# Retention's gated output: its five turnings placed in the seventh and eighth step and in front of the branch projection

## The chip, the cores and the metric

The kernel runs on one core of a Trainium2 chip. The metric is device time in microseconds (us) of one execution. The core has a matrix engine (TensorE, PE in the profile, its weight loads PEld), a vector engine (VectorE, DVE), an activation engine (ScalarE, ACT), GpSimd (POOL) and a queue that issues transfers (SyncE, SP). They run on their own instruction streams, in order, and wait for each other by semaphores. TensorE writes only to PSUM, which has eight banks of 128 partitions x 512 float32; the other engines read the results there and free the bank.

## The reference

One layer of a hybrid encoder trunk: a combined input projection, retention with four heads, differential attention, a mixture of experts. The change touches retention alone, for 512 prompt rows and 8 x 16 sample rows (640 rows, five tiles of 128):

```python
rq, rk = rope(q), rope(k) * RET_DK ** -0.5           # 4 heads, 256 columns each
ret_o, ret_state_new = retention(rq, rk, rv, state)  # 512 value columns per head
ret_o = rms_norm(ret_o) * silu(rg)                   # per head, gated
merged = sigmoid(gates)[ret] * (ret_o @ w_br_ret) + sigmoid(gates)[diff] * (diff_o @ w_br_diff)
```

`ret_o` of a head is 640 x 512. For the product with `w_br_ret` (the branch projection) it must stand with its 512 columns on the partitions, so it is transposed ("turned"), tile by tile. The norm's factor of each row is applied after the product.

## The kernel before

A float32 product is made of three matmuls (`mm3`, L93 to L95) of high and low parts in a rounded format, so each operand is split: ACT makes the high part, another engine the low part. Weights come by DMA into a ring of four pieces of 256 rows (`load_piece`), ACT makes the high part (L628), GpSimd the low part (L546).

`project` multiplies the 640 rows by one group of 512 weight columns: eight steps (one per 128 rows of the contraction), each of five tiles x three matmuls, into the five banks `pj[0]` to `pj[4]`. In front of step i it calls `between(i)`, which issues other work of PE. The stage runs, for each head h: QKh (columns of q and k), then the branch projection of the head before (`BR{h-1}`), then Vh (values), Gh (gate), the products inside the head (`values`) and `state`. For h = 4, the last round, the columns of the merging gate (GR0) stand in the place of QK. BR has two halves "a" and "b" of four steps, each with its own five banks' worth of results, so bank t must be emptied of QK's tile t before the first step of half a touches it (`pj_free`).

Small results of PE go by turns into two scratch banks (`sm`, named r_sm in the trace). They are numbered jobs: a job may start when the job two before it has been taken (`small`, `sm_free`). The list of jobs is written out in `retention_order`, and PE's program must issue them in that order: around the change it is one unit of the modulation (AD), the state products U8 to U15, the five turnings O0 to O4, and two more units inside BR.

While PE runs QK (or GR0), `in_qk` gives it: at step i = 1 a modulation unit and the rest of the sample rows' product with the state (`cross`); at i = 2 to 5 two state products each (`steps`, L1094); at i = 5 behind them turning 0; at i = 6 turnings 1 and 2; at i = 7 turnings 3 and 4. So "the sixth step" is i = 5, "the eighth" i = 7. `turn_o(h, t)` is four transposes of 128 x 128 (L1111) from `gate[:, t]` into one scratch bank. `in_branch` issues a modulation unit at steps 1 and 5 of BR.

DVE takes the state products U (`update`, L853), gates the sample tile, computes the sums for the norm, then `lo_oT` for t = 0 to 4 (L867: the low part of turned tile t, which frees the scratch bank), five small instructions of a reciprocal root, in rounds 1 to 3 the rotation of three tiles of the new q and k, and then `add_branch` (L886, L888), which empties the banks of half a.

ACT's program in a round is an order written out by hand:

```python
split_hi(b, 0)
take_oT(h - 1, 0)
take_oT(h - 1, 1)
act.wait_ge(var_done, h)
act.activation(st[:, 2, 0:NT], st[:, 1, 0:NT], ACT.Sqrt).then_inc(std_done, 1)
split_hi(b, 1)
take_oT(h - 1, 2)
take_oT(h - 1, 3)
split_hi(b, 2)
take_oT(h - 1, 4)
...
take(first, lambda t: qk[:, t].rearrange("p a c -> p (a c)"), ACT.Copy)   # ACT.Sigmoid in the last round
```

`take_oT(h, t)` (L667) is the high part of turned tile t; `take` (L633) empties the five banks of QK (or GR0), tile by tile. The lines L686 to L711 hold this order. SP loads the branch's piece p when QK's piece p has been used. "Second head" is the round with h = 2, from 290 us on; "last head" is the round with h = 4.

Of the kernel before, what the change touches and what calls it, by code (L numbers as in the profile page):

```python
# [41 lines left out]
NP_T = SEQ // P  # L42
# [48 lines left out]
def mm3(pe, out, s_hi, s_lo, m_hi, m_lo, start, stop):  # L91

    pe.matmul(out, s_hi, m_hi, start=start, stop=False)  # L93
    pe.matmul(out, s_hi, m_lo, start=False, stop=False)  # L94
    return pe.matmul(out, s_lo, m_hi, start=False, stop=stop)  # L95
# [102 lines left out]
def phase_r(nc, io, K):  # L198
# [9 lines left out]
    with ExitStack() as ctx:  # L208
# [23 lines left out]
        oT_hi = sb("r_oT_hi", [P, 4, NT * P], F32R)  # L232
        oT_lo = sb("r_oT_lo", [P, 4, NT * P], F32R)
# [81 lines left out]
        def job_taken(eng, *job):  # L315
            eng.wait_ge(sm_free[o.job[job] % 2], o.job[job] // 2 + 1)
# [10 lines left out]
        def bank_taken(eng, name, t):  # L327
            eng.wait_ge(pj_free[t], o.turn[name, t] + 1)
# [621 lines left out]
        def _(pe):  # L950
# [48 lines left out]
            def small(*job):  # L999
                n = o.job[job]  # L1000
                if n >= 2:
                    pe.wait_ge(sm_free[n % 2], n // 2)
                return sm[n % 2]

            def project(name, stat_hi, stat_lo, between):
                parts = [("", range(KT))] if name[:2] != "BR" else [("a", range(4)), ("b", range(4))]
                for part, ks in parts:
                    for k in ks:
                        i = k + (4 if part == "b" else 0)
                        p, kk = i // 2, i % 2  # L1010
                        between(i)
                        if kk == 0:
                            pe.wait_ge(lo_done, o.piece[name, p] + 1)
                        if name == "QK0":
                            pe.wait_ge(h_lo, k + 1)
                        for t in range(NT):
                            if name == "QK0":
                                in_start(k, t)
                            if k == 0:
                                turn = o.turn[name + part, t]  # L1020
                                if turn:
                                    pe.wait_ge(pj_free[t], turn)
                                if part:
                                    job_taken(pe, "O", int(name[-1]), t)
                            s = slice(t * P, (t + 1) * P)
                            last = mm3(pe, pj[t][:], stat_hi[:, k, s], stat_lo[:, k, s], hi[:, p, kk], lo[:, p, kk],
                                       k == 0, k == ks[-1])
                            if k == ks[-1]:
                                last.then_inc(pj_done, 1)
                        if kk and k != ks[-1]:  # L1030
                            last.then_inc(used, 1)

            def unit(u):
                out = small("AD", u)
                pe.wait_ge(u_in, 16 * (u + 1))
                for k in range(KT):
                    j = k % NH
                    last = pe.matmul(out[32 * j:32 * j + 32, 0:UW], cS[:, k], uraw[:, k], start=(k < NH), stop=(k >= KT - NH))
                last.then_inc(sm_done, 1)
# [19 lines left out]
            def values(h, i):  # L1059
                name = f"AV{h}"  # L1060
                if o.turn[name, i]:
                    pe.wait_ge(pj_free[i], o.turn[name, i])
                pe.wait_ge(sc_low, h + 1)
                for j in range(i + 1):
                    bank_taken(pe, f"V{h}", j)
                    b = scoff[j] // P + i - j
                    high = qk_r[:, b // 2, 0, b % 2 * P:(b % 2 + 1) * P]
                    last = mm3(pe, pj[i][:], high, sc_lo[:, b * P:(b + 1) * P], v_hi[:, j], v_lo[:, j], j == 0, j == i)
                last.then_inc(pj_done, 1)
# [8 lines left out]
            def cross(h, q):  # L1078
                d = q // 2
                pe.wait_ge(z_done, h * 5 + d + 1)  # L1080
                pe.wait_ge(S_in[q % 2], 64 * (h * 2 + d + 1))
                for u in range(4 * q, 4 * q + 4):
                    j = strip(u)
                    last = pe.matmul(X[32 * j:32 * j + 32], qz[:, d, stream(u)[1]], S[:, u % 8], start=False, stop=(q == 3))
                if q == 3:
                    last.then_inc(x_done, 1)

            def steps(h, u0):
                pe.wait_ge(vk_in, 128 * (h + 1))
                for u in (u0, u0 + 1):  # L1090
                    (a, s), d = place_of(u), u // DEC_B
                    out = small("U", h, u)
                    k0 = K_AT[s] + d * P
                    pe.matmul(out[:], vk[:, a, k0:k0 + P], vk[:, a, RDK:RDK + RDV], start=True, stop=True).then_inc(sm_done, 1)  # L1094

            def state(h, d):
                out = small("S", h, d)
                pe.wait_ge(kd_low, h + 1)
                for t in range(NP_T):
                    s = slice(d * P, (d + 1) * P)  # L1100
                    last = mm3(pe, out[:], kd_hi[:, t, s], qk_r[:, t, 1, s], v_hi[:, t], v_lo[:, t], t == 0, t == NP_T - 1)
                last.then_inc(sm_done, 1)

            def turn_o(h, t):
                if t < NP_T:
                    bank_taken(pe, f"AV{h}", t)
                else:
                    pe.wait_ge(x_free, h + 1)
                out = small("O", h, t)
                for a in range(4):  # L1110
                    last = pe.transpose(out[:, a * P:(a + 1) * P], gate[:, t, a * P:(a + 1) * P], K.ident[:])  # L1111
                last.then_inc(sm_done, 1)

            def in_start(k, t):
                if k == 0:
                    turned_x(pe, NT + t)
                if (k, t) in ADA_AT:
                    ada(1 + ADA_AT.index((k, t)))
                elif (k, t) in TURN_AT:
                    turn_mod(1 + TURN_AT.index((k, t)))  # L1120

            def in_qk(h, u, i):
                if i == 1:
                    unit(u)
                    cross(h, 2)
                    cross(h, 3)
                elif 2 <= i <= 5:
                    steps(h, 4 + 2 * i)
                if i == 5:
                    turn_o(h, 0)  # L1130
                elif i == 6:
                    turn_o(h, 1)
                    turn_o(h, 2)
                elif i == 7:
                    turn_o(h, 3)
                    turn_o(h, 4)

            def in_branch(u, i):
                if i % 4 == 1:
                    unit(u + i // 4)  # L1140

            def in_v(h, i):
                if i >= 3:
                    turn_qk(h, ROPE_ORDER[i - 3])

            def in_gate(h, u, i):
                if i == 0:
                    scores(h, 4)
                elif i == 1:
                    scores(h, 0)  # L1150
                elif i == 2:
                    sample_values(h)
                    unit(u)
                    cross(h, 0)
                    cross(h, 1)
                    scores(h, 1)
                elif i == 3:
                    scores(h, 2)
                    scores(h, 3)
                elif i >= 5:  # L1160
                    steps(h, 2 * i - 10)
# [12 lines left out]
            u = 0  # L1174
            for h in range(RH + 1):
                if h == 0:
                    project("QK0", *hT, lambda i: None)
                else:
                    project(f"QK{h}" if h < RH else "GR0", *hT, lambda i: in_qk(h - 1, u, i))
                    project(f"BR{h - 1}", oT_hi, oT_lo, lambda i: in_branch(u + 1, i))  # L1180
                    u += 3
                if h == RH:
                    break
                project(f"V{h}", *hT, lambda i: in_v(h, i))
                project(f"G{h}", *hT, lambda i: in_gate(h, u, i))
                u += 1
                for i in range(NP_T):
                    values(h, i)
                    if i == 0:
                        steps(h, 6)  # L1190
                state(h, 0)
                state(h, 1)
# [1879 lines left out]
```

## Time and profile before

| | |
|---|---|
| median of 3 runs | 1493.19 us (1491.91 to 1493.68) |
| the profiled execution's own time | 1492.03 us |
| its span | 1489.8 us |
| PE busy | 1461.5 us (98%) |
| DVE, ACT, POOL busy | 837.7 (56%), 659.5 (44%), 303.2 us (20%) |
| retention stage | from the start to about 700 us of the span |
| waits of PE from 150 to 640 us | 2.8 + 0.6 us, all at L1111 |

Matmuls overlap: each is recorded with 0.39 us, and the next starts 0.23 us after it. So times on PE are read from start to start, and a step of fifteen matmuls is 3.4 us. "[0.71 <-DVE r_S L853]" behind a row is the idle time of the engine before it, and what ended it. "x4" merges four instructions that follow each other.

### The profile page before, as it was taken

How to read it: one execution, taken by the hardware profiler on the slowest of the kernel's cores; microseconds unless marked ns; L12 is line 12 of the kernel's file. 1: busy time of each engine (PE TensorE's matmuls, PEld its weight loads, DVE VectorE, ACT ScalarE, POOL GpSimd, SP SyncE). 2: the span in 40 equal slices, each digit the busy share in tenths (PEclk: the TensorE clock that was granted, in tenths of full speed). 3: DMA queues.
4: the chain of work that ended last, by engine and by line, in shares of the span. 5: the costliest groups of instructions: out<-in, count | busy, mean ns of one | idle time of the engine just before them, and what ended most of it. 6: DMA issues, size and time to landing. Idle time of an engine off the chain costs nothing.

```text
span 1489.8 us, 21889 instructions
## 1 busy us (share of the span) xinstructions
PE 1461.5 (98%) x8004; PEld 1158.5 (78%) x8004; DVE 837.7 (56%) x1456; ACT 659.5 (44%) x1083; POOL 303.2 (20%) x181
## 2 busy tenths in 40 slices
PE   8999999999999999999999999999999999999998
PEld 6777787778777877787877677777888888887885
DVE  3532532253225222221866778655365899988998
ACT  5323312331233123322446545645233478888883
POOL 1352233224313431233000000000321100001004
PEclk9999999999999999999999999999999999999999
DMA  9646565555556455433441353245831799999996
GB/s 324 216 125 204 170 192 140 187 191 184 158 185 208 144 167 197 161 99 91 159 142 43 111 168 133 71 153 178 276 124 43 267 372 404 403 365 402 399 393 230
DMA packets 156460, 304.61 MB, mean 204 GB/s; under 512 B 16752, under 2 KB 54520, under 8 KB 155972
## 3 DMA queue, kind: packets, MB, share of 16 engines
q1 hardware_dynamic: 152548, 292.72, 58.2%
q0 software_dynamic: 3808, 10.49, 2.0%
q8 instruction: 66, 1.08, 0.3%
q14 instruction: 38, 0.31, 0.1%
HBM read 258.45 MB, written 47.86 MB: 206 GB/s over the span
## 4 chain that ended last, share of the span: by engine, by line
PE 45%; DMA 4%; DVE 2%; issue 1%; ACT 1%; POOL 0%; DVEq 0%; ACTq 0%; SPq 0%; POOLq 0%
PE pj L93 11%; PE pj L95 11%; PE pj L94 11%; DMA m_raw<-w 2%; PE d_B L2731 1%; PE d_B L2758 1%; PE d_B L2750 1%; DMA d_kc<-cache_diff_k 1%; PE d_B L2792 1%; PE d_B L2740 1%; PE d_B L2898 1%; PE d_B L2719 1%; PE d_B L1762 1%; PE d_B L2769 0%; PE pj L1745 0%
## 5 line engine op out<-in xcount | busy, mean ns | idle before, releaser
L93 PE MATMUL pj<-ring_hi,hT_hi 128*128 128x512 f32 x880 | 364.1, 414 | 3.7 <-ACT d_q_rows L2193 2.4
L95 PE MATMUL pj<-ring_hi,hT_lo 128*128 128x512 f32 x880 | 345.2, 392 | 0.0
L94 PE MATMUL pj<-ring_lo,hT_hi 128*128 128x512 f32 x880 | 344.0, 391 | 0.0
L546 POOL TENSOR_TENSOR ring_lo<-ring_raw,ring_hi 128x1024 fp32r<-128x1024 f32 x79 | 190.7, 2414 | 462.6 <-ACT ring_hi L628 462.5
L1622 DVE TENSOR_TENSOR m_lo<-m_raw,m_hi 128x1024 fp32r<-128x1024 f32 x188 | 222.1, 1221 | 18.8 <-ACT m_hi L1528 17.3
L628 ACT ACTIVATE ring_hi<-ring_raw 128x1024 fp32r<-128x1024 f32 x79 | 83.5, 1059 | 313.8 <-DMA ring_raw<-w_in 272.8
L1528 ACT ACTIVATE m_hi<-m_raw 128x1024 fp32r<-128x1024 f32 x188 | 192.0, 1058 | 19.9 <-DMA m_raw<-w 17.8
L93 PEld LDWEIGHTS pj<-ring_hi,hT_hi 128*128 128x128 f32 x880 | 166.2, 189 | 41.8 <-issue 8.9
L95 PEld LDWEIGHTS pj<-ring_hi,hT_lo 128*128 128x128 f32 x880 | 165.4, 188 | 36.1
L94 PEld LDWEIGHTS pj<-ring_lo,hT_hi 128*128 128x128 f32 x880 | 166.4, 189 | 29.3 <-issue 1.0
L853 DVE SCALAR_TENSOR_TENSOR r_S<-r_S,g,r_sm 128x512 f32<-128x512 f32 x64 | 45.0, 745 | 128.4 <-PE r_sm L1094 128.4
L93 PE MATMUL pj<-m_hi,m_xT_hi 128*128 128x512 f32 x248 | 98.4, 397 | 0.8 <-DVE m_lo L1622 0.8
L95 PE MATMUL pj<-m_hi,m_xT_lo 128*128 128x512 f32 x248 | 96.9, 391 | 0.0
L94 PE MATMUL pj<-m_lo,m_xT_hi 128*128 128x512 f32 x248 | 96.6, 390 | 0.0
L2186 ACT ACTIVATE ring_hi<-ring_raw 128x1024 fp32r<-128x1024 f32 x37 | 39.1, 1058 | 66.4 <-DMA ring_raw<-w_in 27.2
L1492 POOL DMA_INDIRECT m_xe<-xg,m_si x16 | 19.8, 1239 | 229.0 <-PE d_B L1754 209.6
L93 PE MATMUL pj<-ring_hi,r_oT_hi 128*128 128x512 f32 x160 | 63.4, 396 | 0.0
L94 PE MATMUL pj<-ring_lo,r_oT_hi 128*128 128x512 f32 x160 | 62.5, 391 | 0.0
L95 PE MATMUL pj<-ring_hi,r_oT_lo 128*128 128x512 f32 x160 | 62.3, 389 | 0.0
L841 DVE COPY r_qkT<-r_sm 128x512 f32<-128x512 f32 x20 | 13.8, 691 | 75.9 <-PE r_sm L1045 75.9
L93 PEld LDWEIGHTS pj<-m_hi,m_xT_hi 128*128 128x128 f32 x248 | 46.6, 188 | 11.1 <-DVE m_lo L1622 2.0
L95 PEld LDWEIGHTS pj<-m_hi,m_xT_lo 128*128 128x128 f32 x248 | 46.6, 188 | 9.9
(403 smaller groups left out, 2507.4 us busy)
## 6 DMA issues: line engine op xcount, KB each, us to landing
m_raw<-w SPq DMA_DIRECT2D x188, 512.0 KB, 9.8
ring_raw<-w_in SPq DMA_DIRECT2D x72, 512.0 KB, 3.8
r_S<-state_ret SPq DMA_DIRECT2D x64, 256.0 KB, 4.7
r_ada_raw<-w_ada SPq DMA_DIRECT2D x16, 1024.0 KB, 6.6
o_state_s<-r_S SPq DMA_DIRECT2D x64, 256.0 KB, 3.3
a_raw<-w_ada SPq DMA_DIRECT2D x16, 512.0 KB, 8.7
ring_raw<-w_in SPq DMA_DIRECT2D x32, 256.0 KB, 3.4
ring_raw<-w_br_ret SPq DMA_DIRECT2D x16, 512.0 KB, 4.5
```

What stands on the lines that cost most here:

```text
L93: pe.matmul(out, s_hi, m_hi, start=start, stop=False)
L94: pe.matmul(out, s_hi, m_lo, start=False, stop=False)
L95: return pe.matmul(out, s_lo, m_hi, start=False, stop=stop)
L546: pool.tensor_tensor(lo[:, p], raw[:, p], hi[:, p].bitcast(F32), ALU.subtract).then_inc(lo_done, 1)
L628: act.activation(hi[:, p], raw[:, p], ACT.Copy).then_inc(hi_done, 1)
L853: dve.scalar_tensor_tensor(S[:, u % 8], S[:, u % 8], K.g16[:, h:h + 1], job_bank("U", h, u)[:], ALU.mult, ALU.add) \
L1492: pool.indirect_dma_start(out=self.xe[e % 2][:], out_offset=None, in_=self.io["xg"][0:NT * P, :], in_offset=bass.IndirectOffsetOnAxis(ap=s ...
L1528: act.activation(self.hi[self.slot(n)][:], self.raw[self.slot(n)][:], ACT.Copy).then_inc(self.hi_done, 1)
L1622: dve.tensor_tensor(self.lo[s][:], self.raw[s][:], self.hi[s][:].bitcast(F32), ALU.subtract).then_inc(self.lo_done, 1)
L1762: last = pe.transpose(self.AT[:, a * P:(a + 1) * P], self.su[:, a * P:(a + 1) * P], K.ident[:])
L2186: act.activation(hi[:, p], raw[:, p], ACT.Copy).then_inc(hi_done, 1)
L2719: last = pe.transpose(out[:, h * P:(h + 1) * P], rows[a][:, t, h * P:(h + 1) * P], K.ident[:])
```

## The change

Turning 0 moves from step 5 to step 6, together with turning 1; turnings 2 and 3 stand at step 7; turning 4 stands in front of the first step of the branch projection. The order of all jobs in the scratch banks stays. The programs of ACT, DVE, GpSimd and SP are not touched.

```diff
                     cross(h, 3)
                 elif 2 <= i <= 5:
                     steps(h, 4 + 2 * i)
-                if i == 5:
-                    turn_o(h, 0)
-                elif i == 6:
-                    turn_o(h, 1)
-                    turn_o(h, 2)
-                elif i == 7:
-                    turn_o(h, 3)
-                    turn_o(h, 4)
-
-            def in_branch(u, i):
-                if i % 4 == 1:
+                if i >= 6:
+                    turn_o(h, 2 * i - 12)
+                    turn_o(h, 2 * i - 11)
+
+            def in_branch(h, u, i):
+                if i == 0:
+                    turn_o(h, NP_T)
+                elif i % 4 == 1:
                     unit(u + i // 4)
...
-                    project(f"BR{h - 1}", oT_hi, oT_lo, lambda i: in_branch(u + 1, i))
+                    project(f"BR{h - 1}", oT_hi, oT_lo, lambda i: in_branch(h - 1, u + 1, i))
```

## Rows read from the trace of the kernel before

**Rows 1.** The page's first lines: span; busy time per engine

```profile
span 1489.8 us, 21889 instructions
PE 1461.5 (98%) x8004; PEld 1158.5 (78%) x8004; DVE 837.7 (56%) x1456; ACT 659.5 (44%) x1083; POOL 303.2 (20%) x181
```

**Rows 2.** Waits of PE, 150 to 640 us: waiter, releaser, us in total, times, longest

```profile
PE r_sm L1111 <- DVE r_S L853: 2.8, 4, 0.7
PE r_sm L1111 <- DVE r_oT_lo L867: 0.6, 4, 0.2
```

**Rows 3.** PE in order of time, second head: start, duration, line, shape, [idle before]

```profile
304.69 0.62 PE L1094 MATMUL r_sm<-r_vk 128*128 128x512 f32 x2
...
308.54 0.61 PE L1094 MATMUL r_sm<-r_vk 128*128 128x512 f32 x2
309.86 0.63 PE L1111 MATMUL r_sm<-ident,r_gate 128*128 128x128 f32 x4 [0.71 <-DVE r_S L853]
...
313.78 1.03 PE L1111 MATMUL r_sm<-ident,r_gate 128*128 128x128 f32 x8
...
318.07 0.60 PE L1111 MATMUL r_sm<-ident,r_gate 128*128 128x128 f32 x4
318.83 0.63 PE L1111 MATMUL r_sm<-ident,r_gate 128*128 128x128 f32 x4 [0.16 <-DVE r_oT_lo L867]
319.22 0.47 PE L93 MATMUL pj<-ring_hi,hT_hi 128*128 128x512 f32 x1
319.53 0.39 PE L94 MATMUL pj<-ring_lo,hT_hi 128*128 128x512 f32 x1
...
322.73 0.39 PE L93 MATMUL pj<-ring_hi,r_oT_hi 128*128 128x512 f32 x1
```

**Rows 4.** The page's group of state updates: busy, mean ns; idle before

```profile
L853 DVE SCALAR_TENSOR_TENSOR r_S<-r_S,g,r_sm 128x512 f32<-128x512 f32 x64 | 45.0, 745 | 128.4 <-PE r_sm L1094 128.4
```

**Rows 5.** ACT in order of time, second head

```profile
318.71 0.60 ACT L667 ACTIVATE r_oT_hi<-r_sm 128x512 fp32r<-128x512 f32 x1 [0.74 <-PE r_sm L1111]
...
320.15 0.59 ACT L667 ACTIVATE r_oT_hi<-r_sm 128x512 fp32r<-128x512 f32 x1
320.63 2.90 ACT L633 ACTIVATE r_qk<-pj 128x512 f32<-128x512 f32 x5
```

**Rows 6.** DVE in order of time, second head

```profile
320.77 0.69 DVE L867 TENSOR_TENSOR r_oT_lo<-r_sm,r_oT_hi 128x512 fp32r<-128x512 f32 x1 [0.74 <-ACT r_oT_hi L667]
...
335.07 1.43 DVE L888 SCALAR_TENSOR_TENSOR acc_ret<-pj,r_st,acc_ret 128x512 f32<-128x512 f32 x2 [2.99 <-PE pj L95]
```

**Rows 7.** PE in order of time, last head

```profile
598.06 0.61 PE L1094 MATMUL r_sm<-r_vk 128*128 128x512 f32 x2
...
612.27 0.47 PE L93 MATMUL pj<-ring_hi,r_oT_hi 128*128 128x512 f32 x1
```

**Rows 8.** ACT in order of time, last head

```profile
609.67 0.59 ACT L667 ACTIVATE r_oT_hi<-r_sm 128x512 fp32r<-128x512 f32 x1
610.28 1.28 ACT L633 ACT_TABLE_LOAD   x1
611.58 2.56 ACT L633 ACTIVATE r_qk<-pj 128x512 f32<-128x512 f32 x5
```

**Rows 9.** PE around the phase's end, in order of time

```profile
696.28 0.39 PE L95 MATMUL pj<-ring_hi,hT_lo 128*128 128x512 f32 x1
699.06 0.50 PE L93 MATMUL pj<-ring_hi,hT_hi 128*128 128x512 f32 x1 [2.39 <-ACT d_q_rows L2193]
...
700.09 0.49 PE L94 MATMUL pj<-ring_lo,hT_hi 128*128 128x512 f32 x1
...
703.74 0.39 PE L94 MATMUL pj<-ring_lo,hT_hi 128*128 128x512 f32 x1
```

**Rows 10.** Windows: stretch, busy of PE, PEld, DVE, ACT, POOL; granted clock; DMA

```profile
700.50:703.50 3.00, 3.00 (x9) 2.33 (x8) 0.00 (x0) 2.38 (x4) 0.00 (x0) 0.50 0.64 211
...
1352.00:1356.00 4.00, 2.68 (x13) 1.84 (x11) 3.94 (x5) 3.37 (x4) 0.00 (x0) 1.00 1.05 412
```

## The prediction

> **What bounds the kernel now.** I read the page's busy times first. PE is busy 1461.5 of 1489.8 us, DVE 56% [rows 1], so a change to retention counts only by what it does to PE's stream of matmuls. Then PE's waits over the retention stage: only two kinds, both in front of the turnings at L1111, four times each (once per head): 0.71 us for the state update that frees the scratch bank of the first turning, 0.16 us for the low half of the third turned tile in front of the fifth turning [rows 2]. Last, the order of time on PE, ACT and DVE around the turnings, in the second head and in the last one. The four heads repeat one pattern: 14.19 us from the last pair of L1094 to the branch projection in the second [rows 3], 14.21 us in the last [rows 7].
>
> **Part 1: turning 0 leaves the sixth step.** A step with a pair of state products and no turning takes 308.54 - 304.69 = 3.85 us. The sixth, with turning 0, takes 313.78 - 308.54 = 5.24 us [rows 3]. After the change it is a plain one: 1.39 us saved a head. The pair's banks are free when the seventh step starts: the update that PE waited for was over by 309.86 and the other takes 0.75 us more [rows 4], which makes 310.6, against a seventh step at 308.54 + 3.85 = 312.39. So the 0.71 us wait is not moved but gone.
>
> **Part 2: the seventh and eighth steps.** The seventh holds two turnings before and after. It takes 318.07 - 313.78 = 4.29 us, with no wait [rows 3]. The eighth holds two now too, with the wait between them: 322.73 - 318.07 = 4.66 us. Its pair becomes 2 and 3. They need banks of tiles 0 and 1, turned one step (4.29 us) earlier. A low half is done some 2 us after its turning starts (PE 318.07, ACT 318.71, DVE right after, 0.69 us), so neither waits. The eighth step drops to 4.29 us: 0.37 us saved. Together 1.76 us a head; the branch projection could start at 322.73 - 1.76 = 320.97 us, were nothing put in front of it. Of the 1.76, about 0.44 us is work of one turning that is only moved (4.29 less 15 matmuls at the spacing of (322.73 - 319.53)/14 = 0.229, which is 3.43, halved), and 1.3 us is waiting and its run-up, that goes.
>
> **Part 3: turning 4 in front of the branch projection.** The four transposes are nothing; what matters is who stands behind them. The first branch matmul writes bank 0, which still holds the projected tile 0 of q and k (the gate, in the last head). ACT empties the banks with L633, and in ACT's program L633 stands behind the copy of turned tile 4. Before, that copy starts at 320.15 and L633 at 320.63 [rows 5], while PE is still in the eighth step, and the branch starts at 322.73 with the usual spacing: cover of about 1.4 us. The change takes that cover away: the copy can't start until the turning in front of the branch is done. Chain from 320.97:
> - turning to ACT's copy, 318.71 - 318.07 = 0.64 us [rows 3, 5];
> - copy to L633, 320.63 - 320.15 = 0.48 us [rows 5];
> - L633 to the first branch matmul: the second head doesn't show it, since PE isn't waiting there. The last head does: 612.27 - 611.58 = 0.69 us [rows 7, 8], where PE starts just as the first tile is out.
>
> Sum 1.81: the first branch matmul at 322.78. After a turning the first two matmuls start 0.31 us apart (319.22, 319.53) instead of 0.23 [rows 3], which adds 0.08. Net 322.86 against 322.73: **+0.13 us a head**, so what the two waits gave back is spent on the new one. Bounds: the last link can't be under the 0.60 us of ACT's own instruction, and I allow as much above 0.69, 0.78; the other two links 0.05 in all. Per head 0.0 to +0.25; in the last +1.3 to +1.6. The other tiles don't wait: ACT's spacing is at most 2.90/5 = 0.58 us a tile, PE wants one each 0.68 us.
>
> **Part 4: the last head has a table load.** There L633 is a sigmoid, and ACT loads its table after the copy of tile 4: copy 609.67, load 610.28 (1.28 us), sigmoid 611.58 [rows 8]. Even now that is just in time. After: turning at 612.27 - 1.76 = 610.51; copy +0.64 = 611.15; to the load 0.61, to the sigmoid 1.30, to PE 0.69: 613.75 us, against 612.27: **+1.48 us**. The slow first spacing is in the before of this head already.
>
> ScalarE's load stands in the row at 1.28 us, with the sigmoid 0.02 us behind it. The Trainium skill (ScalarE: Activation LUTs, What ACT_TABLE_LOAD costs) prices a switch at 1.28 us of load plus about 1.38 us of drain. By the rule the sum of the last head would be 2.9 us instead of 1.5; I take the row, which has the load start 0.02 us after the end of the copy at 610.26, and no drain.
>
> **What is behind it on other engines.** DVE's low half of tile 4 comes after ACT's copy, now at about 322.2 instead of 320.77, with the reciprocal root and three rotations queued behind. DVE idles 2.99 us before the first branch sum at 335.07 [rows 6], so a delay of 1.5 us is hidden, with 1.5 left; in the last head it has no rotations there at all. If that cover were gone, the second half of the projection would wait by what is over. The fifth tile of the first branch step needs that low half at 322.86 + 4 x 0.68 = 325.6; it is there at 322.9. ACT's own queue has two weight pieces to split (about 1 us each) between the turnings; both fit into the 4.29 us of a step. SP loads the branch's third and fourth pieces when steps six and eight have been used, so 1.4 and 1.8 us earlier, and nothing of its queue moves behind anything new. GpSimd gets its pieces no later.
>
> **Sum.** 3 x 0.13 + 1.48 = +1.9 us (1.3 to 2.4 by the bounds). The profiled execution: span 1489.8, time 1492.03, so 2.2 us lie around the span. Its span would be 1491.7, its time 1493.9. The median of three runs is 1493.19, 1.2 above the profiled one; on it the forecast is 1495.1 us.
>
> **Rivals.**
> *A. The clock falls in the last head: slower.* From the end of the turning (610.51 + 0.60) to 613.75, PE is idle for 2.64 us. At the end of the phase PE idles 2.39 us before 699.06, and one microsecond later the granted clock is 0.50 (1.2 of 2.4 GHz) for some three microseconds [rows 9, 10]. The nine matmul spacings from 700.09 to 703.74 take 3.65 us instead of 9 x 0.229 = 2.06: 1.6 us lost. The same in the last head gives 1.9 + 1.6 = +3.5, 1496.7 us. For it: the new gap is longer than the one that did it. Against: that is one case, and whether a gap does it may be luck. In the other heads the gap is 322.78 - 321.57 = 1.2 us; in a stretch with 4.00 - 2.68 = 1.32 us of idle PE the clock stayed at 1.00 [rows 10], so none there. It decides the sign if the gap of 2.64 us is treated as the one of 2.39 was. The Trainium skill (TensorE: Matmul & The Clock Gate, Part 1: The HAM clock gate) has the clock throttled by default and released by activity, and at half clock counts half of the throttled time as lost: of the 3.00 us in the row 1.5, an estimate.
>
> *B. The first branch tile does not wait: faster.* If ACT empties bank 0 before the turned tile 4, or its chain is much shorter than its rows say, only the gain is left: 4 x 1.3 = 5.2 us, 1488.0. Against it stands ACT's written order. This is the reading that a mere count of PE's waits would give.
>
> *C. A worse price behind the turning: slower.* The table switch costs a drain when the copy before it comes late, +1.4 us, 1496.5; or DVE's 1.5 us of cover doesn't do and each of the first three heads loses up to a microsecond, 1497.
>
> **How the numbers follow.** Forecast 0.50, A 0.33, C 0.11, B 0.06. What can be told from no change is about 0.2%, 3.0 us, so the lines are at 1490.2 and 1496.2. The forecast lies under the upper line by 1.1 us, and the run-to-run spread shown is 1.8 us, so I give 0.06 of its 0.50 to slower. A gives 0.27 to slower and 0.06 to same, C 0.09 and 0.02. Slower 0.42, same 0.52, faster 0.06. The forecast's own range is 1493.8 to 1496.4; the range with A and C, and the spread, is 1492.6 to 1498.2; it leaves out B and the far ends.
>
> **What would show it.** In the new trace: no idle PE before the first turning (now two in the seventh step) and none before the pair of the eighth; a new wait of PE, four times, on ACT L633, about 1.2 us in three heads and 2.6 in the last; the table load of the last head between copy and sigmoid, uncovered; DVE's idle time before the branch sums down by about 1.5 us; and from last L1094 to branch 14.3 us in three heads and 15.7 in the last. A clock of 0.50 right after the last head's branch start is A. I am wrong if PE starts the branch less than 1.5 us after the turning starts (B), or if a wait shows up that is none of these.

## The result

Over 19 runs of the changed kernel against 20 of the kernel before, the changed kernel takes 1.0026 of the time, 95% interval 1.0019 to 1.0032: slower by 3.9 us (2.8 to 4.8). The medians are 1495.29 and 1491.95 us. One more run of the changed kernel, at 3754.94 us, stood far outside and is left out of both. A second comparison, 12 runs against 23, gave 1.0020 (1.0011 to 1.0029).

The profiled execution took 1495.24 us, its span is 1493.0 (before 1489.8, [rows 1]). PE's waits in the page of the changed kernel, the longest first; in the whole span, those of less than 2 us left out:

```profile
PE pj L93 <- issue: 5.2, 3, 2.6
PE pj L954 <- ACT a_c L593: 4.2, 1, 4.2
PE d_B L2737 <- DVE d_o L2466: 3.1, 4, 1.1
PE pj L93 <- POOL ring_lo L546: 2.4, 2, 1.2
PE pj L93 <- ACT d_q_rows L2190: 2.4, 1, 2.4
```

The two waits at L1111 of [rows 2] are gone. New is PE's wait in front of the branch projection, L93, at most 2.6 us in one place. The profile names GpSimd's low half in two heads and nothing ("issue") in the others; the third wait under "issue", 1.3 us at 26.19, is in the kernel before too. PE in order of time in the second head, to be read against [rows 3]:

```profile
304.77 0.62 PE L1094 MATMUL r_sm<-r_vk 128*128 128x512 f32 x2
...
308.63 0.62 PE L1094 MATMUL r_sm<-r_vk 128*128 128x512 f32 x2
309.08 0.39 PE L93 MATMUL pj<-ring_hi,hT_hi 128*128 128x512 f32 x1
...
312.49 1.04 PE L1111 MATMUL r_sm<-ident,r_gate 128*128 128x128 f32 x8
...
316.78 1.03 PE L1111 MATMUL r_sm<-ident,r_gate 128*128 128x128 f32 x8
...
321.08 0.60 PE L1111 MATMUL r_sm<-ident,r_gate 128*128 128x128 f32 x4
322.90 0.47 PE L93 MATMUL pj<-ring_hi,r_oT_hi 128*128 128x512 f32 x1 [1.22 <-issue]
323.20 0.39 PE L94 MATMUL pj<-ring_lo,r_oT_hi 128*128 128x512 f32 x1
```

PE idles 1.22 us in front of the branch. The sixth step takes 3.86 us, the seventh and eighth 4.29 and 4.30; then the turning at 321.08 and the branch at 322.90. ACT in the same stretch:

```profile
317.42 1.09 ACT L667 ACTIVATE r_oT_hi<-r_sm 128x512 fp32r<-128x512 f32 x2 [0.74 <-PE r_sm L1111]
319.56 1.06 ACT L628 ACTIVATE ring_hi<-ring_raw 128x1024 fp32r<-128x1024 f32 x1 [1.05 <-DMA ring_raw<-w_br_ret]
321.71 0.60 ACT L667 ACTIVATE r_oT_hi<-r_sm 128x512 fp32r<-128x512 f32 x1 [1.09 <-PE r_sm L1111]
322.21 2.55 ACT L633 ACTIVATE r_qk<-pj 128x512 f32<-128x512 f32 x5
```

From start to start it is 0.63 us from the turning to ACT's copy, 0.50 from there to L633, and 0.69 to PE's branch. The last head, PE and then ACT ([rows 7, 8]):

```profile
598.52 0.62 PE L1094 MATMUL r_sm<-r_vk 128*128 128x512 f32 x2
...
610.97 0.60 PE L1111 MATMUL r_sm<-ident,r_gate 128*128 128x128 f32 x4
614.21 0.47 PE L93 MATMUL pj<-ring_hi,r_oT_hi 128*128 128x512 f32 x1 [2.64 <-issue]
614.52 0.58 PE L94 MATMUL pj<-ring_lo,r_oT_hi 128*128 128x512 f32 x1
614.90 0.63 PE L95 MATMUL pj<-ring_hi,r_oT_lo 128*128 128x512 f32 x1
...
617.89 0.44 PE L93 MATMUL pj<-ring_hi,r_oT_hi 128*128 128x512 f32 x1
618.16 0.39 PE L94 MATMUL pj<-ring_lo,r_oT_hi 128*128 128x512 f32 x1
```

```profile
611.61 0.60 ACT L667 ACTIVATE r_oT_hi<-r_sm 128x512 fp32r<-128x512 f32 x1 [2.26 <-PE r_sm L1111]
612.22 1.28 ACT L633 ACT_TABLE_LOAD   x1
613.52 2.56 ACT L633 ACTIVATE r_qk<-pj 128x512 f32<-128x512 f32 x5
```

The table load stands behind the copy, the sigmoid 0.02 us behind the load, and PE 0.69 us behind the sigmoid. Then the matmuls start 0.43 us apart instead of 0.23, for three microseconds: the clock has fallen. Windows of the two stretches at half clock, behind the last head and behind the end of the phase (columns as in [rows 10]):

```profile
614.80:617.80 3.00, 3.00 (x8) 2.35 (x8) 0.00 (x0) 2.21 (x4) 0.71 (x1) 0.50 0.03 5
703.50:706.00 2.50, 2.50 (x8) 1.91 (x7) 0.00 (x0) 1.77 (x4) 0.13 (x1) 0.50 0.89 285
```

| us, from the traces | before | changed |
|---|---|---|
| last L1094 to branch, first head | 14.18 | 14.27 |
| second | 14.19 | 14.27 |
| third | 14.21 | 14.28 |
| last | 14.21 | 15.69 |
| first five tiles of the branch, first three heads | 3.49 | 3.61 |
| the same, last head | 3.60 | 5.20 |
| last matmul of the phase, start | 696.28 | 699.80 |

The first four rows of the table are counted from the start of the last pair of L1094 to the start of the branch; the "first five tiles" are its first 15 matmuls. The four heads make 0.09 + 0.08 + 0.07 + 1.48 = 1.72 us, the first tiles behind them 3 x 0.12 + 1.60 = 1.96: together 3.68. The phase ends 3.52 us later, and had started 0.13 us earlier, so that is all of it. The rest of the span gives 0.3 us back.

### The profile page after: what moved, and what is told of

It reads as the page before. It is cut to its first block, busy times and chain, and to the rows that moved or that the text cites. A ratio compares the mean times of both kernels' runs of the same rounds, so it can differ in the third digit from the quotient of the medians.

```text
span 1493.0 us, 21889 instructions
## 1 busy us (share of the span) xinstructions
PE 1461.4 (98%) x8004; PEld 1160.3 (78%) x8004; DVE 832.2 (56%) x1456; ACT 660.0 (44%) x1083; POOL 303.5 (20%) x181
## 4 chain that ended last, share of the span: by engine, by line
PE 46%; DMA 3%; DVE 2%; issue 1%; ACT 1%; POOL 0%; DVEq 0%; ACTq 0%; POOLq 0%; SPq 0%
PE pj L93 12%; PE pj L95 11%; PE pj L94 11%; PE d_B L2728 1%; DMA m_raw<-w 1%; PE d_B L2755 1%; PE d_B L2747 1%; PE d_B L2789 1%; DMA d_kc<-cache_diff_k 1%; PE d_B L2737 1%; PE d_B L2895 1%; PE d_B L2716 1%; PE d_B L2766 1%; DMA m_xe<-xg,m_si 1%; PE d_B L1759 1%
## 5 line engine op out<-in xcount | busy, mean ns | idle before, releaser
L93 PE MATMUL pj<-ring_hi,hT_hi 128*128 128x512 f32 x880 | 363.7, 413 | 3.7 <-ACT d_q_rows L2190 2.4
L93 PEld LDWEIGHTS pj<-ring_hi,hT_hi 128*128 128x128 f32 x880 | 166.1, 189 | 41.7 <-issue 8.9
L93 PE MATMUL pj<-m_hi,m_xT_hi 128*128 128x512 f32 x248 | 98.2, 396 | 1.4 <-DVE m_lo L1619 1.4
L93 PE MATMUL pj<-ring_hi,r_oT_hi 128*128 128x512 f32 x160 | 64.2, 401 | 6.3 <-issue 3.9
L93 PEld LDWEIGHTS pj<-m_hi,m_xT_hi 128*128 128x128 f32 x248 | 46.6, 188 | 11.4 <-DVE m_lo L1619 2.3
```

## The experiments

**Is the new wait ACT's order of work?** The first three banks are emptied before the copy of turned tile 4:

```diff
                     split_hi(b, 2)
+                    func = ACT.Copy if h < RH else ACT.Sigmoid
+                    take(first, lambda t: ..., func, ts=range(3))
                     take_oT(h - 1, 4)
...
-                    take(first, lambda t: ..., ACT.Copy)
+                    take(first, lambda t: ..., ACT.Copy, ts=rest)
```

> The changed kernel, but ACT empties the first three banks of the projection (L633) before it copies turned tile 4, instead of after it. Theory 1 (the new wait is ACT's written order: turned tile 4, then bank 0): the wait in front of the branch projection goes in all four heads, last pair of L1094 to branch falls from 14.27 us (15.69 in the last head) to 14.19 - 1.76 + 0.47 = 12.9 us, the table load of the last head falls into ACT's idle time, the clock stays full there. 4 x 1.3 = 5.2 us under the kernel before, some 8.7 under the changed one: ratio to before 0.9965. Theory 2 (PE waits there for the low half of the branch's first weight piece, as the profile names GpSimd in two heads): nothing changes, ratio 1.002 to 1.003.

Measured: 0.9954 of the time before (0.9942 to 0.9967), median 1486.45 us, five runs. From last L1094 to branch 12.81, 12.80, 12.80 and 12.84 us. ACT in the last head:

```profile
604.26 1.06 ACT L628 ACTIVATE ring_hi<-ring_raw 128x1024 fp32r<-128x1024 f32 x1
605.35 1.28 ACT L633 ACT_TABLE_LOAD   x1
606.64 1.58 ACT L633 ACTIVATE r_qk<-pj 128x512 f32<-128x512 f32 x3
608.09 0.62 ACT L667 ACTIVATE r_oT_hi<-r_sm 128x512 fp32r<-128x512 f32 x1
608.56 1.12 ACT L633 ACTIVATE r_qk<-pj 128x512 f32<-128x512 f32 x2
```

The load starts at 605.35, while PE is still in the eighth step; the branch starts at 607.34. PE has no wait there, and the granted clock is 1.00:

```profile
607.40:612.00 4.60, 4.60 (x34) 3.13 (x32) 1.46 (x6) 3.35 (x6) 0.40 (x1) 1.00 0.35 118
```

Theory 2 falls: the same pieces, split by the same engine at the same places of its program, keep nobody waiting once bank 0 is free. And GpSimd in the changed kernel, second head, had done the low half of the branch's first piece long before PE wanted it at 322.90:

```profile
302.59 2.40 POOL L546 TENSOR_TENSOR ring_lo<-ring_raw,ring_hi 128x1024 fp32r<-128x1024 f32 x1 [20.20 <-ACT ring_hi L628]
```

So "POOL ring_lo" in the list of waits names a semaphore that PE also waits for, not the one that was late. The last matmul of the phase starts at 691.35, 4.93 us before that of [rows 9], and the phase had begun 0.27 us later: 5.2 us, as expected. The runs' ratio says 6.9 (4.9 to 8.7); the excess is within its interval. This kernel beats the kernel before and the changed one.

**Is the last head's loss the table load, and what does the clock take?** One element's sigmoid in front of the copy, in the last head:

```diff
                     split_hi(b, 2)
+                    if h == RH:
+                        act.activation(st[0:1, 4, 7:8], K.ident[0:1, 0:1], ACT.Sigmoid)
                     take_oT(h - 1, 4)
```

> The changed kernel with one more instruction of ACT in the last head alone: a sigmoid of one element in front of the copy of turned tile 4, so that the table load falls before it. Theory 1: last head from 15.69 to 14.3 us, and with the shorter idle time of PE (1.2 us instead of 2.6) the clock does not fall there: 1.4 + 1.6 = 3.0 us less than the changed kernel, so 0.5 us above the kernel before, ratio 1.0003. If the clock has nothing to do with that gap: 1.4 us less, ratio 1.0014. If the table load costs a drain beside its 1.28 us: up to 2.8 us less without the clock.

Measured: 1.0003 (0.9991 to 1.0014), 12 runs. The last head takes 14.27 us instead of 15.69, 1.42 less, and its first five tiles 3.61 instead of 5.20. ACT:

```profile
609.49 1.28 ACT L702 ACT_TABLE_LOAD   x1
610.78 0.20 ACT L702 ACTIVATE r_st<-ident 1x1 f32<-1x1 f32 x1
611.73 0.60 ACT L667 ACTIVATE r_oT_hi<-r_sm 128x512 fp32r<-128x512 f32 x1 [0.74 <-PE r_sm L1113]
612.22 2.55 ACT L633 ACTIVATE r_qk<-pj 128x512 f32<-128x512 f32 x5
```

The load is over before the turning is done, and L633 follows the copy by 0.49 us as in the other heads. The 1.42 us are the load (1.28), the 0.03 us at its two ends, and some 0.1 by which two ACTIVATEs that follow each other overlap (0.49 us from start to start, 0.60 each); no room is left for a drain. The clock stayed full there.

**Is it the idle PE that the clock falls for?** Ten matmuls more, in the time in which PE waits:

```diff
                 if i == 0:
                     turn_o(h, NP_T)
+                    if h == RH - 1:
+                        for _ in range(10):
+                            pe.matmul(X[:, 0:P], K.ident[:], K.ident[:], start=True, stop=True)
```

> The changed kernel with ten more matmuls of 128 x 128 (about 0.23 us each, results never read) behind turning 4 in the last head, where PE waits anyway. Theory 1: the branch starts as late as in the changed kernel (15.7 us), but the granted clock stays 1.00 behind it: 1.6 us less than the changed kernel, +2.0 us on the kernel before, ratio 1.0013. Rival (the clock's fall was chance in the profiled run and makes no difference on the whole): as the changed kernel, ratio 1.0023 to 1.0026. Second rival (more work on PE costs what it takes): 2 us more, 1.004.

Measured: 1.0014 (1.0004 to 1.0024), 12 runs. One of the 12, the longest at 1500.58 us, has a mean clock of 0.948; no trace shows where it lost it. PE around the added matmuls, which the profile records as 20:

```profile
611.12 0.60 PE L1111 MATMUL r_sm<-ident,r_gate 128*128 128x128 f32 x4
611.56 2.40 PE L1138 MATMUL r_X<-ident 128*128 128x128 f32 x20
614.37 0.47 PE L93 MATMUL pj<-ring_hi,r_oT_hi 128*128 128x512 f32 x1 [0.41 <-issue]
614.67 0.40 PE L94 MATMUL pj<-ring_lo,r_oT_hi 128*128 128x512 f32 x1
614.91 0.40 PE L95 MATMUL pj<-ring_hi,r_oT_lo 128*128 128x512 f32 x1
```

```profile
614.40:618.00 3.60, 3.60 (x19) 2.70 (x19) 0.00 (x0) 2.76 (x5) 0.76 (x1) 1.00 0.04 12
```

The branch is as late as in the changed kernel (15.70 us), and the clock is full behind it: the first tiles take 3.61 us instead of 5.20. In this place more work on PE takes less time, 1.6 us in the traces; in the runs it is 1.0014 against 1.0026 and 1.0020, where the intervals overlap, so the times alone do not show it. The span of this profile, 1494.3 us, is even longer than the changed kernel's. Up to the last matmul of the phase it is ahead (698.39 against 699.80 us); then PE's wait at the phase's end is 0.8 us longer (3.19 against 2.35), and what follows that wait takes 1.9 us more, which no run explains.

**Does the order pay without the moved turnings?** The kernel before, with ACT's new order:

```diff
                     split_hi(b, 2)
+                    take(first, ..., ts=range(3))
                     take_oT(h - 1, 4)
```

> The kernel before, with ACT's order alone changed as in the first of these runs (three banks, then turned tile 4). Theory 1: PE does not wait for bank 0 in the kernel before, so nothing is gained in three heads and 0.03 us in the last: ratio 1.000, and only with the moved turnings does the order pay. Rival (the order is worth something by itself, and the gain of the first run is no proof of the wait): ratio under 0.998.

Measured: 1.0003 (0.9994 to 1.0012), 11 runs; 14.17 to 14.20 us in all heads. So the gain of the first experiment needs both the order and the moved turnings.

**Part 3 alone.** The edit is against the changed kernel: turnings 0 to 3 go back to where the kernel before has them.

```diff
-                if i >= 6:
-                    turn_o(h, 2 * i - 12)
-                    turn_o(h, 2 * i - 11)
+                if i == 5:
+                    turn_o(h, 0)
+                elif i == 6:
+                    turn_o(h, 1)
+                    turn_o(h, 2)
+                elif i == 7:
+                    turn_o(h, 3)
```

> Part 3 of the change alone: turnings 0, 1 and 2, 3 where the kernel before has them, turning 4 in front of the branch projection. Theory 1: sixth step 5.24 us as before, seventh 4.29, eighth with one turning 3.43 + 0.47 = 3.9, then 1.82 us of wait chain: 15.25 us from last L1094 to branch in three heads, 16.67 in the last, +0.13 for slower first spacings in three, 1.6 for the clock in the last. 3 x 1.2 + 2.5 + 1.6 = +7.6 us on the kernel before, ratio 1.0051. Rival (the moved turning costs nothing, the changed kernel's loss comes from the regrouping): ratio 1.000.

Measured: 1.004 (1.0026 to 1.0053), six runs. 15.23, 15.23, 15.23 and 16.65 us, within 0.02 of the expected; the expected ratio, 1.0051, lies inside the interval. In this profile the clock was low for twice as long behind the last head (the first tiles took 6.46 us instead of 3.60), again behind 2.64 us of idle PE:

```profile
615.33 0.60 PE L1111 MATMUL r_sm<-ident,r_gate 128*128 128x128 f32 x4
618.57 0.77 PE L93 MATMUL pj<-ring_hi,r_oT_hi 128*128 128x512 f32 x1 [2.64 <-issue]
619.13 0.63 PE L94 MATMUL pj<-ring_lo,r_oT_hi 128*128 128x512 f32 x1
```

But at the end of the phase the clock did not fall here, though PE idled 2.32 us before 708.15. The first experiment has the same 2.32 us of idle PE there, before 694.06, and it did fall. The stretches behind the two, first experiment and then this one (columns as in [rows 10]):

```profile
694.10:697.10 3.00, 3.00 (x7) 2.42 (x8) 0.00 (x0) 2.37 (x5) 0.98 (x2) 0.50 0.87 242
708.15:712.00 3.85, 3.85 (x17) 3.20 (x18) 0.00 (x0) 2.99 (x6) 1.03 (x2) 1.00 0.72 202
```

So the length of the idle time alone does not decide it; what else does is open.

**Parts 1 and 2 alone.** Again against the changed kernel: turning 4 goes back into the eighth step.

```diff
                 if i >= 6:
                     turn_o(h, 2 * i - 12)
                     turn_o(h, 2 * i - 11)
+                if i == 7:
+                    turn_o(h, NP_T)
...
-                if i == 0:
-                    turn_o(h, NP_T)
-                elif i % 4 == 1:
+                if i % 4 == 1:
```

> Parts 1 and 2 alone: turnings 0 and 1 at step seven, 2, 3 and 4 at step eight, none in front of the branch. Theory 1: the sixth step falls to 3.85 us, but turning 4 waits in the eighth for the low half of tile 2, done 2.09 us after turning 2 starts: eighth step 2.09 + 0.39 + 3.50 = 5.98 instead of 4.66 us. 3.85 + 4.29 + 5.98 = 14.12 us against 14.19: -0.07 us a head, no wait in front of the branch, clock full, ratio 0.9998. Rival (the two waits of the kernel before are gone by the regrouping alone): 12.9 us a head, ratio 0.9965.

Measured: 0.9993 (0.9985 to 1.0002), 12 runs; 14.15 to 14.17 us a head. What the sixth step gains is lost again in the eighth, in a wait in front of turning 4:

```profile
316.73 1.03 PE L1111 MATMUL r_sm<-ident,r_gate 128*128 128x128 f32 x8
318.83 0.63 PE L1111 MATMUL r_sm<-ident,r_gate 128*128 128x128 f32 x4 [1.07 <-DVE r_oT_lo L867]
319.21 0.48 PE L93 MATMUL pj<-ring_hi,hT_hi 128*128 128x512 f32 x1
```

Turning 4 follows turning 2 too closely and waits 1.07 us, where it waited 0.16 before [rows 3]. With turning 4 in the eighth step the regrouping gives next to nothing (14.19 to 14.16 us in the second head); with turning 4 in front of the branch it gives 0.96 us a head (15.23 in part 3 alone to 14.27 in the changed kernel).

**The changed kernel again.**

> The changed kernel again, beside the other two on the same chip. Theory 1: 14.27 us from last L1094 to branch in three heads, 15.69 in the last, clock at 0.50 behind it, +3.6 us on the kernel before, ratio 1.0024. Rival (the clock's fall was chance in the first profile): clock full behind the last head, +2.0 us, ratio 1.0013.

Measured: 1.0020 (1.0011 to 1.0029), 12 runs; 14.27, 14.27, 14.28 and 15.69 us, the first tiles of the last head 5.03 us, at half clock again. The mean clock of a run bears it out beyond the profiles: 0.9969 over the 19 runs of the changed kernel and 0.9971 over these 12, against 0.9985 over the kernel before's, 0.9988 with the table load early, 0.9988 over the five runs with the banks first, and 0.9985 over 11 of the 12 runs with PE kept busy (without the one at 0.948). The difference of 0.0015 between the changed kernel and the one before is 2.3 us of lost clock, somewhat more than one stretch of three microseconds at half. This, more than the times, bears out the third experiment over many runs. One of the 12 runs of this repetition has 0.999, so the clock is not lost every time.

## Why the prediction was right, and where it was not

**Parts 1 and 2** came out as worked out: 3.86, 4.29 and 4.30 us against 3.85, 4.29 and 4.29, neither with a wait.

**Part 3's chain** was forecast at 0.64 + 0.48 + 0.69 and measured at 0.63 + 0.50 + 0.69; the link that the second head did not show was rightly taken from the last head's row. +0.13 us a head was forecast, 0.05 up to the branch and 0.08 for the slow start behind a turning; the traces have 0.08 and 0.12, 0.20 in all. Both terms are a little small, together 0.2 us in three heads.

**Part 4**: +1.48 forecast, 1.48 measured, and the second experiment puts 1.42 of it to the load and what goes with it. The drain of the Trainium skill's rule (ScalarE: Activation LUTs, What ACT_TABLE_LOAD costs) does not show: the trace has 0.02 us on either side of the load.

**The clock** is where the forecast's case was wrong. Rival A, which had 0.33, is what happened: 1.9 + 1.6 = 3.5 us was its sum, and the traces have 3.7, the runs 3.9 and 3.0. The failed step is the weighing: "that is one case, and whether a gap does it may be luck" kept the 1.6 us out of the likeliest sum, though the gap of 2.64 us was longer than the 2.39 us one that had lost the clock in the only profile at hand. The runs showed that it is lost nearly always: in both profiles of the changed kernel, in that of part 3 alone, and by the mean clock of 31 runs. The doubt itself was not empty, as the two idle times of 2.32 us with different outcomes show; it was given too much weight. That the time named, 1495.1, stands 0.2 us from the measured median is luck: the change was put at +1.9 us and measured at +3.9 and +3.0, and the median of the three runs that the forecast was counted from was 1.2 us above that of the 20.

The Trainium skill (TensorE: Matmul & The Clock Gate, Part 1: The HAM clock gate) says that the throttled state is the default and activity releases it. The third experiment agrees: the same delay with PE busy keeps 1.00.

**Rival B** (only the gain is left, 5.2 us) is the first experiment: it needed another order in ACT's program, and without that did not come; it had been given 0.06. **Rival C** did not come: no drain shows, and DVE kept 2.72 us of idle time before the branch sums.

**What was said of the other engines** held in its conclusion, not in its numbers. DVE's idle time before the branch sums was to fall by 1.5 us and fell from 2.99 to 2.72; where the rest went is told in the last section. And ACT's third weight piece was to fit without trouble: it was not there in time. SP issued its load at 314.78, behind four stores, and not 1.4 us before 313.97; ACT waited 1.05 us for it (319.56) and was done with the piece 1.1 us before the copy. Had it come over 1.1 us later, it would have been in the chain.

## What to carry to other kernels

A small job put between two stages can cost more than its own time, namely that of the queue behind its reader: here four transposes brought a wait of 1.22 us. Look which instruction of the reading engine stands behind the copy and who waits for it, and change that order with the move (here two kernels that differ in that order alone have spans of 1493.0 and 1484.4 us). Where a wait on PE grows, add up not only the wait: the table load on the chain added itself in full, and an idle PE of 2.64 us was paid for twice, the second time by the clock. In a chain of jobs with two banks, the wait that went from turning 0 turned up at turning 4 as long as that one had not moved too.

## What the runs showed that was not expected

DVE's second small instruction of the reciprocal root takes 1.17 us in the kernel before and 0.17 in the changed one. DVE and GpSimd of the kernel before, then of the changed one:

```profile
321.59 1.17 DVE L117 TENSOR_TENSOR r_st<-r_st 128x5 f32<-128x5 f32 x1
322.80 0.17 DVE L119 TENSOR_TENSOR r_st<-r_st 128x5 f32<-128x5 f32 x1
```

```profile
320.33 2.40 POOL L546 TENSOR_TENSOR ring_lo<-ring_raw,ring_hi 128x1024 fp32r<-128x1024 f32 x1 [0.39 <-ACT ring_hi L628]
```

```profile
323.17 0.17 DVE L117 TENSOR_TENSOR r_st<-r_st 128x5 f32<-128x5 f32 x1
```

```profile
320.70 2.37 POOL L546 TENSOR_TENSOR ring_lo<-ring_raw,ring_hi 128x1024 fp32r<-128x1024 f32 x1 [1.54 <-ACT ring_hi L628]
```

Before, it starts while GpSimd subtracts (320.33 to 322.73) and ends with it, at 322.76; in the changed kernel DVE comes 1.6 us later, when GpSimd is done (323.07), and is not held up. So the later copy cost DVE 1.6 us and gave 1.0 back; with the branch sums starting 0.3 us later (335.37 against 335.07), that leaves the 0.27 us by which DVE's idle time fell. No run was made for this by itself, but the nine profiles have 36 heads, and they agree. In eight (all four of the kernel before and of parts 1 and 2 alone) the instruction starts while GpSimd subtracts; there it takes 0.94 to 1.17 us and ends 0.02 to 0.03 us after GpSimd does. In the other 28 it starts when GpSimd is idle and takes 0.17 us. The Trainium skill (SBUF — State Buffer, Terms) has the two engines share a port pair that one of them holds for a whole instruction; these rows agree.

The other surprise is how often one short idle time of PE costs the clock: 2.64 us of it did in all three profiles that have it, once for twice the usual stretch; the 2.3 to 3.2 us at the end of the phase did in eight of the nine; and the 1.2 us of the other heads did in none.
